# A third pair of chunks as seven block products, two of its block sums by accumulating transfers

## The reference

```python
def _swiglu(x, wg, wu, wd):
    return (jax.nn.silu(x @ wg) * (x @ wu)) @ wd
...
for l in range(DEPTH_2):
    g = norm_g[l]
    h = _swiglu(_rmsnorm(x, g[0]), ffn_w_gate[l, 0], ffn_w_up[l, 0], ffn_w_down[l, 0])
    x = x + 0.5 * _rmsnorm(h, g[1])
    ...
    h = _swiglu(_rmsnorm(x, g[4]), ffn_w_gate[l, 1], ffn_w_up[l, 1], ffn_w_down[l, 1])
    x = x + 0.5 * _rmsnorm(h, g[5])
```

## Time and profile before

| | us |
|---|---|
| median of 3 runs | 1287.07 |
| lowest, highest | 1286.22, 1288.68 |
| the profiled execution | 1285.86 |
| its span | 1284.1 |
| TensorE busy | 1263.2 |
| VectorE busy | 925.0 |
| ScalarE busy | 714.3 |
| GpSimd busy | 137.8 |

### The profile page before, as it was taken

One profiled execution on the slowest core, in us unless ns is written; L12 is line 12 of the kernel. 1 busy time (PEld: TensorE's weight loads), 2 busy tenths in 40 slices (PEclk: granted clock), 3 DMA queues, 4 the chain that ended last, 5 costly groups with the idle time before them and its releaser, 6 DMA issues.

```text
span 1284.1 us, 17130 instructions
## 1 busy us (share of the span) xinstructions
PE 1263.2 (98%) x6807; PEld 1039.2 (81%) x6807; DVE 925.0 (72%) x969; ACT 714.3 (56%) x902; POOL 137.8 (11%) x120
## 2 busy tenths in 40 slices
PE   8999999999989999999999999999999999999998
PEld 6887888887778888877788887888887887788886
DVE  4477767555888885676887866887856687887874
ACT  4433644444646564746646557555647655746553
POOL 3000199000570000010000000000000200000000
PEclk9999999999999999999999999999999999999999
DMA  9996486655395536562766354946263544675351
GB/s 335 379 401 219 168 267 221 195 188 188 101 347 175 164 105 240 184 195 66 272 201 215 99 200 145 329 131 228 91 222 129 165 147 132 223 268 190 106 175 70
DMA packets 160762, 252.92 MB, mean 197 GB/s; under 512 B 9336, under 2 KB 111028, under 8 KB 160692
## 3 DMA queue, kind: packets, MB, share of 16 engines
q1 hardware_dynamic: 157696, 243.28, 56.5%
q0 software_dynamic: 2624, 8.48, 1.7%
q10 hardware_dynamic: 372, 0.19, 0.1%
HBM read 248.73 MB, written 1.05 MB: 195 GB/s over the span
## 4 chain that ended last, share of the span: by engine, by line
PE 86%; ACT 5%; DVE 5%; DMA 2%; SPq 1%; issue 1%; DVEq 0%; ACTq 0%
PE ps L742 19%; PE ps L744 19%; PE ps L743 19%; PE ps L841 5%; PE ps L950 4%; PE ps L951 4%; PE ps L954 4%; PE ps L838 3%; PE ps L790 1%; DVE w_lo L2120 1%; PE ps L1337 1%; PE ps L782 1%; PE ps L783 1%; ACT xT_pair L1576 1%; PE ps L766 1%
## 5 line engine op out<-in xcount | busy, mean ns | idle before, releaser
L2120 DVE TENSOR_TENSOR w_lo<-raw,w_hi 128x2048 fp32r<-128x2048 f32 x163 | 374.1, 2300 | 92.0 <-ACT w_hi L1521 91.2
L1521 ACT ACTIVATE w_hi<-raw 128x2048 fp32r<-128x2048 f32 x163 | 310.9, 1911 | 145.4 <-PE ps L744 80.5
L742 PE MATMUL ps<-w_lo,xT_pair 128*128 128x512 f32 x436 | 173.4, 398 | 0.9 <-DVE w_lo L2120 0.9
L744 PE MATMUL ps<-w_hi,xT_pair 128*128 128x512 f32 x436 | 170.2, 390 | 0.0
L743 PE MATMUL ps<-w_hi,xT_pair 128*128 128x512 f32 x436 | 169.8, 390 | 0.0
L742 PE MATMUL ps<-w_lo,hT_hi 128*128 128x512 f32 x400 | 157.3, 393 | 3.1 <-DVE hT_lo L2335 2.7
L744 PE MATMUL ps<-w_hi,hT_lo 128*128 128x512 f32 x400 | 155.8, 390 | 0.0
L743 PE MATMUL ps<-w_hi,hT_hi 128*128 128x512 f32 x400 | 155.8, 390 | 0.0
L742 PE MATMUL ps<-xT_pair,w_hi 128*128 128x256 f32 x368 | 107.6, 292 | 0.2 <-DVE xT_pair L2502 0.2
L743 PE MATMUL ps<-xT_pair,w_hi 128*128 128x256 f32 x368 | 104.0, 283 | 0.0
L744 PE MATMUL ps<-xT_pair,w_lo 128*128 128x256 f32 x368 | 104.0, 283 | 0.0
(11 more groups left out here) (333 smaller groups left out, 2296.8 us busy)
## 6 DMA issues: line engine op xcount, KB each, us to landing
raw<-in_ffn_w_down SPq DMA_DIRECT2D x88, 512.0 KB, 4.5
raw<-in_ffn_w_gate SPq DMA_DIRECT2D x56, 512.0 KB, 4.0
raw<-in_ffn_w_up SPq DMA_DIRECT2D x56, 512.0 KB, 5.1
raw<-in_ffn_w_in SPq DMA_DIRECT2D x44, 512.0 KB, 4.7
arena<-in_ffn_w_up SPq DMA_DIRECT2D x32, 512.0 KB, 5.9
raw<-in_conv_w_in SPq DMA_DIRECT2D x24, 512.0 KB, 9.6
raw<-in_fox_w_in SPq DMA_DIRECT2D x24, 512.0 KB, 4.6
raw<-in_ffn_w_out SPq DMA_DIRECT2D x22, 512.0 KB, 4.2
```

The lines of the kernel that those rows point to most:

```text
L742: pe.matmul(o, a_hi, b_lo, start=first, stop=False, skip_group_check=True)
L744: return pe.matmul(o, a_lo, b_hi, start=False, stop=last, skip_group_check=True)
L1521: act.activation(w_hi[:, slot_of(n), :], raw[:, raw_slot(n), :], ACT.Copy).then_inc(hi_ready, 1)
L2120: dve.tensor_tensor(w_lo[:, slot_of(n), :], source(n), w_hi[:, slot_of(n), :].bitcast(F32), ALU.subtract).then_inc(raw_done, 1)
```

## The change

Each of the four stages gets a third pair. Chunks 0, 1, 2, 5 and 10 stay by rows; the pairs are chunks 3 and 4, 6 and 7, 8 and 9. The stage has 42 units: 21 block products for 14, ten half chunks for fourteen, eleven down units as before. The first pair begins at unit 8, not 11. After it come chunk 5 (units 16, 17), the second pair (19, 21 to 23, 25 to 27) and, with nothing in between, the third (28, 29, 31, 32, 34 to 36, with down units 30 and 33 inside), then chunk 10 (37, 38) and three down units.

The sums T3 of the second and third pair and T4 of the third are made by accumulating transfers from GpSimd's queue (`add_blocks`); the other nine (`VECTOR_SUMS`) stay on VectorE. T4 of the first two pairs is now written to xn. The loads follow the new order; among them the second half of chunk 2 (unit 6) is issued ahead of the wait for `x_new` and of the first blocks. `turned` of the chunk before the last goes to yT, not to hT.

```diff
-QUAD_AT = ({11: Q_B21, 12: Q_B11, 13: Q_T1, 14: Q_T2, 16: Q_T3, 17: Q_B22, 18: Q_T4},
-           {22: Q_B21, 24: Q_B11, 25: Q_T1, 26: Q_T2, 28: Q_T3, 29: Q_B22, 30: Q_T4})
+QUAD_AT = ({8: Q_B21, 9: Q_B11, 10: Q_T1, 11: Q_T2, 13: Q_T3, 14: Q_B22, 15: Q_T4},
+           {19: Q_B21, 21: Q_B11, 22: Q_T1, 23: Q_T2, 25: Q_T3, 26: Q_B22, 27: Q_T4},
+           {28: Q_B21, 29: Q_B11, 31: Q_T1, 32: Q_T2, 34: Q_T3, 35: Q_B22, 36: Q_T4})
...
+VECTOR_SUMS = ((0, Q_T1), (0, Q_T2), (0, Q_T3), (0, Q_T4), (1, Q_T1), (1, Q_T2), (1, Q_T4), (2, Q_T1), (2, Q_T2))
...
(SyncE, load_seven)
-                half_chunk(5, 2, 0)
+                chunk(5, 2)
                 sp.wait_ge(x_new, x_count(s - 1, 1, 1))
                 block(0, 0)
-                half_chunk(6, 2, 1)
                 block(1, 0)
                 down_rows(7, 1)
                 block(2, 0)
-                half_chunk(8, 3, 0)
                 block(3, 0)
...
+                sp.wait_ge(raw_done, n + 22)
+                block(0, 2)
+                half_chunk(37, 10, 0)
+                sp.wait_ge(sum_ok, sum_count(s, 1, Q_T4))
+                block(3, 2)
+                sp.wait_ge(raw_done, n + 26)
+                block(1, 2)
+                sp.wait_ge(raw_done, n + 27)
+                block(2, 2)
...
(TensorE, seven)
+                def fill_third(i):
+                    if i == 0:
+                        pe.wait_ge(quad_hid, 2 * pair_no(s, 1) + 2)
+                        turn_pair(1, 0)
+                    if i == 1:
+                        down(30, 6)
+                        turn_pair(3, 1)
+                    if i == 2:
+                        down(33, 7)
+
+                pair(2, (28, 29, 31, 32, 34, 35, 36), 0, 2, 1, fill_third)
...
(GpSimd)
+            def add_blocks(s):
+
+                n = BASE[s]
+                for p in (1, 2):
+                    pool.wait_ge(sum_ok, sum_count(s, p, Q_T1))
+                    pool.wait_ge(quad_landed[1], 32 * (pair_no(s, p) + 1))
+                    pool.dma_start(b_12, b_22, accum_op=ALU.add).then_inc(t3_landed, 16)
+                pool.wait_ge(sum_ok, sum_count(s, 2, Q_T2))
+                pool.wait_ge(raw_done, n + 29)
+                pool.dma_start(b_21, t_2, accum_op=ALU.add).then_inc(t4_landed, 16)
```

More of the change, by code:

```diff
@@ L277, in block_program @@
         t_1, t_2 = [b[:, :, :].rearrange("p t d -> p (t d)") for b in (tmp, xn)]
-        quad_src = {Q_B21: b_21, Q_B11: b_11, Q_T1: t_1, Q_T2: t_2, Q_T3: b_12, Q_B22: b_22, Q_T4: b_21}
+        quad_src = {Q_B21: b_21, Q_B11: b_11, Q_T1: t_1, Q_T2: t_2, Q_T3: b_12, Q_B22: b_22}
         s_1, u_2 = part(9216, 512), part(9728, 512)
@@ L436, in source, with sum_count, t3_count @@
         def source(n):
-            return quad_src[QUAD_OF[n][1]] if n in QUAD_OF else raw[:, raw_slot(n), :]
+            if n not in QUAD_OF:
+                return raw[:, raw_slot(n), :]
+            p, q = QUAD_OF[n]
+            return quad_src[q] if q != Q_T4 else (b_21 if p == 2 else t_2)
         def pair_no(s, p):
-            return 2 * SEVEN.index(s) + p
+            return 3 * SEVEN.index(s) + p
+        def sum_count(s, p, q):
+            return len(VECTOR_SUMS) * SEVEN.index(s) + VECTOR_SUMS.index((p, q)) + 1
+        def t3_count(s, p):
+            return 16 * (2 * SEVEN.index(s) + p)
         def row_count(s, c):
@@ L1059, in seven @@
                 pe.wait_ge(hT_ok, NCH * (f + 1) - 1)
-                down_part(last - 1, hT_hi, hT_lo, 0, 0, False, False, ks=(0,))
+                down_part(last - 1, yT_hi, yT_lo, 2, 0, False, False, ks=(0,))
                 pe.wait_ge(hid_done, 2 * row_count(s, 10) + 2)
                 turn_rows(1)
-                down_part(last - 1, hT_hi, hT_lo, 0, 0, False, False, ks=(1,))
+                down_part(last - 1, yT_hi, yT_lo, 2, 0, False, False, ks=(1,))
                 pe.wait_ge(hT_ok, NCH * (f + 1))
@@ L1065, in seven @@
                 down_part(last, yT_hi, yT_lo, 0, 0, False, True).then_inc(y_tok0, 1)
-                down_part(last - 1, hT_hi, hT_lo, 0, 1, False, False).then_inc(w_used, 1)
+                down_part(last - 1, yT_hi, yT_lo, 2, 1, False, False).then_inc(w_used, 1)
                 down_part(last, yT_hi, yT_lo, 0, 1, False, True, ks=(0,))
@@ new lines, in seven @@
+                row_gates(5, 17, (3, 0))
+                hi(20, 21)
+                turned(4, 2)
+                hi(22, 23)
+                copy(21, 3, s_1)
+                turned(5, 2)
+                hi(24)
+                copy(22, 0, s_5)
+                hi(25)
+                silu_first(1)
+                copy(23, 3, u_2)
+                hi(26, 27)
+                copy(25, 3, u_3)
+                hi(28, 29)
+                silu_second(1, 27, 3)
+                hi(30)
+                turned(6, 1)
@@ L2464, in seven @@
+                sum_first(2)
+                turned(6, 1)
+                lo(30)
+                sum_second(2)
+                lo(31)
+                turned(7, 3)
+                lo(32, 33)
+                c_11(2, 2)
+                lo(34, 35, 36)
+                c_22(2)
+                lo(37)
+                c_12(2, 35, 1)
+                pair_hidden(2, 0)
+                pair_hidden(2, 1)
+                lo(38)
+                turned(8, 1)
+                lo(39)
                 if s == FFN3:
-                    dve.wait_ge(w_used, n + 31)
+                    dve.wait_ge(w_used, n + 36)
@@ L2943, in _ @@
             o.then_inc(tap_w_ok, 1)
+            add_blocks(FFN2)
+            add_blocks(FFN3)
             for i in range(FOX_H // 2):
```

265 lines of the change are left out of this document (121 added, 144 removed).

## The result

The changed kernel takes 1303.44 us (median of 6 runs, 1301.74 to 1308.35); the kernel before, beside it, 1288.26 us (6 runs, 1286.22 to 1291.15). The ratio is 1.0122, 95% interval 1.0100 to 1.0143: some 15 us slower. Forecast were +8.3 us, 1295.4 us. The profiled execution of the changed kernel is the longest of its six: 1308.35 us, span 1306.6, mean granted clock 0.989 (the other five: 0.992 to 0.994).

The account below looks back on a forecast made before the run. TensorE, busy 98% of the span, was taken as the bound. Four stages' waits less savings (+8.6 us), FFN1's head (-0.3) and transfers (0) gave +8.3 us on 1287.07, so 1295.4 us, range 1283 to 1306.

Parts of the forecast that it names:

- Part 1, the products: TensorE, each stage: 96 matmuls become 84, saving 2.72 us a stage, 10.9 us in all.
- Part 2, the walk: Third pair, VectorE's queue: TensorE waits 3.10, 0.71, 1.29 us at units 30, 32, 33; net +2.15 us a stage.
- Part 3, the head: FFN1's head: earlier load 6 and moved sum_first(0) start unit 7 at 372.4 against 372.64, -0.3 us; free in FFN2 to FFN4.
- The slack of 1.5 us: Heads of FFN2 to FFN4: hT_lo 1 has about 1.5 us to spare even behind sum_first(0).
- Part 4, the transfers: GpSimd's queue: accumulating transfers of 1 MB land in 8 to 17 us within 18.9 us of room, costing 0.
- The sum: Whole kernel: 8.6 - 0.3 + 0 = +8.3 us, giving 1295.4 us.
- The pace of 0.2265 us: TensorE: matmuls of 512 columns start 0.2265 us apart, so a full unit takes 5.44 us, a block product 2.72.
- The saving comes through: Rival, third pair: w_lo 30 done by t + 5.9 shrinks later waits; 1275.0 us, chance 0.15 for gain wholly or mostly.
- One wait only: Rival, third pair: only unit 30's wait stays, +0.15 us a stage, 1287.4 us; chance 0.13.
- The transfers land late: Rival, unit 34 waits for transfers beyond 18.9 us: 1321.4 or about 1397 us; chance 0.11, including loads in their way.

Follow-up runs that it names:

- e1: Changed kernel plus 12 matmuls of 128 columns with unused results just before down unit 30 in all four stages; 1298.13 us, ratio 1.0082.
- e6: Changed kernel with sum_first(2) behind w_lo 30, hT_hi 7 ahead of w_hi 33, sum_first(0) back behind hT_lo 1; 1284.53 us, ratio 0.9966.
- e11: Changed kernel with only the load of down unit 7 issued ahead of block 1 on SyncE; 1299.46 us, ratio 1.0076.
- e4: Changed kernel without its three accumulating transfers a stage, products using plain blocks (output not the reference's); 1303.62 us, ratio 1.0112.
- e2: Changed kernel with VectorE's sum_first(2) moved behind w_lo 30 instead of ahead of hT_lo 6; 1292.83 us, ratio 1.0039.
- e5: Changed kernel with sum_first(2) behind w_lo 30 on VectorE and hT_hi 7 ahead of w_hi 33 on ScalarE; 1283.38 us, ratio 0.9969.
- the best version: Changed kernel with sum_first(2), hT_hi 7, sum_first(0) and load 7 moved, and the first pair's third sum by transfer; 1279.62 us, ratio 0.9932.

## Why the prediction was wrong

**Part 1, the products.** Right: 48 matmuls of 512 columns fewer.

**Part 2, the walk.** Right in place, order and cause, and in size within 0.3 us each: 4.6 us of waits a stage measured, 5.1 walked. VectorE's idle time ahead of hT_lo 7 in FFN2 was 6.68 us, not 3.9: the slow unit 30 added 2.7. In e1, where unit 30 keeps its pace, it is as walked:

```profile
748.81 0.69 DVE L2367 TENSOR_TENSOR hT_lo<-ps,hT_hi 128x512 fp32r<-128x512 f32 x1 [3.98 <-ACT hT_hi L1759]
```

VectorE's added work, 10.5 us a stage in the prediction, is not the sum of the parts named beside it (three w_lo, a sum and ten small operations are about 15); the pages' busy times differ by 45.9 us, 11.5 a stage. Nothing in the walk rests on it.

**Part 3, the head.** In FFN1 unit 7 started at 373.52, or 371.8 without the shift of 1.7 us that came before the stage; forecast were 372.4. "In FFN2 to FFN4 hT_lo 1 is needed later than it comes ... so the move is free there" is false in two of three stages. Load 6, now ahead of block 0, holds it back on SyncE until 632.8 us, so that blocks 0 and 1 are still on their way when load 7 is issued at 634.98. w_hi 7 waits for its load, and w_lo 7 for w_hi 7:

```profile
646.52 1.92 ACT L1539 ACTIVATE w_hi<-raw 128x2048 fp32r<-128x2048 f32 x1 [1.86 <-DMA raw<-in_ffn_w_down]
...
648.47 2.29 DVE L2151 TENSOR_TENSOR w_lo<-raw,w_hi 128x2048 fp32r<-128x2048 f32 x1 [2.90 <-ACT w_hi L1539]
...
656.01 0.50 PE L761 MATMUL ps<-w_lo,hT_hi 128*128 128x512 f32 x1 [0.65 <-DVE hT_lo L2366]
```

That is 0.65 and 0.59 us, small. The slack of 1.5 us was worked out with w_hi 7 as early as in the kernel before; the sum took it down to that, and the later load, some 2 us, used up the rest (e6 and e11 each take one of the two away, and the wait goes).

**Part 4, the transfers.** Right: 0. They landed in 7.7 us (b_12 += b_22), just under the 8 to 17 us taken, and 11.7 us (b_21 += t_2), against 18.9 us of room, and e4 shows no cost. Issues from GpSimd's queue, KB each, median us to landing:

```profile
arena<-arena POOLq DMA_DIRECT2D x8, 1024.0 KB, 7.7
...
rows<-xn POOLq DMA_DIRECT2D x4, 1024.0 KB, 11.7
```

**The sum: the step that failed.** "4 x 2.15 = 8.6" has the waits alone. It lacks a term for what TensorE's clock does behind them, which the prediction puts at nothing without saying why: 10.3 us at four units 30 and one unit 7 in the profiled run, and some 5 us at the units 30 between the medians (e1). The pace of 0.2265 us was taken from a stretch where TensorE never stopped, and applied to units that follow a stop of 3 us. The rows held a warning that I read as reassurance: the old wait of 2.71 us at unit 7 has full pace behind it, in one execution. e2 shows a wait of 2.67 us at the same place with the pace at 0.427 us from the fifth matmul on:

```profile
371.86 0.50 PE L761 MATMUL ps<-w_lo,hT_hi 128*128 128x512 f32 x1 [2.67 <-DVE hT_lo L2366]
372.19 0.40 PE L762 MATMUL ps<-w_hi,hT_hi 128*128 128x512 f32 x1
372.43 0.39 PE L763 MATMUL ps<-w_hi,hT_lo 128*128 128x512 f32 x1
...
372.94 0.63 PE L762 MATMUL ps<-w_hi,hT_hi 128*128 128x512 f32 x1
```

In hindsight, with that term and the two heads: 8.3 + 1.2 + 10.3 = 19.8 us for the profiled run, where 22.5 were measured, 1.7 of them a fall ahead of FFN1; and 8.3 + 1.2 + 5 = 14.5 us between the medians, where 15.2 were measured. The waits that were forecast are there; the clock is what makes the result nearly twice as large.

**The rivals.** "The saving comes through" was built on the right point: it gave 1275.0 for sum_first(2) out of w_lo 30's way. e2 did that and got 1292.8, since the other waits did not shrink; e5, with ScalarE's order mended as well, is the first to gain. "One wait only" did not come, and "The transfers land late" is refuted by their landing times and by e4.

## What to carry to other kernels

In the feed-forward parts here, a wait of TensorE of 1.9 us or more cost its length and, 24 times out of 28, a spell at half clock: count 1.3 to 2.8 us beside it. Waits of up to 1.2 us there cost their length alone, so splitting a long wait in two is worth a try. Don't take the length for the whole rule: elsewhere in the same kernel a shorter wait had a fall behind it and a longer one had none (the list below). Where the mean load of an engine is 75% and its orders are written by hand, walk the queue behind each new join: here two moved operations turned +1.2% into -0.3%. Take the price of an effect that comes and goes from several runs, not from one trace. And test the parts apart: half of the best version's gain needed no new scheme at all.
